# Query and key projection in other banks and with later rotary partners, and eight low halves per mixer on VectorE

## What is computed

```python
def encoder_layer(x, pos, past, lw):
    x = half_step_ffn(x, ...)
    h = rms_norm(x, lw['mix_norm_pre'])
    m, new_state = hybrid_mixer(h, pos, past, ...)
    x = x + rms_norm(m, lw['mix_norm_post'])
    x = half_step_ffn(x, ...)
    return x, new_state

def hybrid_mixer(...):
    a, g, q, k, v, qi, ki, wi = split_cols(h @ w_in)
    q = apply_rope(q, cos, sin)         # also k, qi, ki
    conv_out = conformer_conv(a, g, ...)       # a * sigmoid(g), depthwise conv, layer norm, silu
    attn_out = sparse_attention(q, qi, wi, pos, k_all, v_all, ki_all)  # top-k keys by an index score
    return concat(conv_out, attn_out) @ w_out

def apply_rope(x, cos, sin):
    x1, x2 = x[..., :half], x[..., half:]
    return concat([x1 * c - x2 * s, x2 * c + x1 * s])
```

## Time and profile before

| | us |
|---|---|
| median of 3 timed runs | 1326.3 |
| lowest, highest | 1325.33, 1329.6 |
| the profiled execution | 1322.26 |
| its span, first to last instruction | 1320.5 |
| busy in it: TensorE, VectorE, ScalarE, GpSimd | 1268.5, 790.9, 606.4, 235.6 |
| mean granted clock of TensorE | 0.982 |

### The profile page before, as it was taken

The page is one execution under the profiler, slowest core; times in us unless marked ns, Lnnn a source line. Parts: engine busy times, 40 slices in busy tenths (PEclk is TensorE's granted clock), DMA queues, the critical chain, the costliest instruction groups (busy, mean ns, idle before and its releaser), DMA issues.

```text
span 1320.5 us, 24629 instructions
## 1 busy us (share of the span) xinstructions
PE 1268.5 (96%) x9533; PEld 1197.8 (91%) x9533; DVE 790.9 (60%) x1408; ACT 606.4 (46%) x998; POOL 235.6 (18%) x150
## 2 busy tenths in 40 slices
PE   5999999998998999999999999999899899999998
PEld 4999999988757899999989999998895599999997
DVE  3666554788325776664487665457961458666543
ACT  3544444542437554444345444444423465444432
POOL 6000000455501600000040000015653062000000
PEclk9999999999989899999999999999999999999998
DMA  6354554446501355445425555453472043544541
GB/s 183 129 191 159 178 175 150 154 129 180 163 1 43 128 176 174 159 151 176 154 95 192 160 177 182 159 172 125 141 202 65 1 138 97 191 161 161 170 155 59
DMA packets 186102, 189.84 MB, mean 144 GB/s; under 512 B 9348, under 2 KB 181644, under 8 KB 186030
## 3 DMA queue, kind: packets, MB, share of 16 engines
q1 hardware_dynamic: 185230, 188.20, 44.8%
q0 software_dynamic: 416, 0.51, 0.2%
q10 hardware_dynamic: 384, 0.13, 0.0%
HBM read 179.21 MB, written 3.93 MB: 139 GB/s over the span
## 4 chain that ended last, share of the span: by engine, by line
PE 76%; DVE 10%; issue 5%; POOL 5%; ACT 2%; DMA 1%; POOLq 0%; DVEq 0%; ACTq 0%; SPq 0%
PE ps L1154 23%; PE ps L1156 22%; PE ps L1155 22%; POOL wlo L1080 5%; PE ps L1397 3%; DVE acc L761 2%; DVE x L782 2%; DVE hl L747 2%; DVE upd L774 1%; DVE wlo L737 1%; PE ps L1462 1%; ACT whi L421 1%; PE ps L1176 1%; PE ps L1432 1%; PE ps L1553 1%
## 5 line engine op out<-in xcount | busy, mean ns | idle before, releaser
L1154 PE MATMUL ps<-hh,wlo 128*128 128x288 f32 x1920 | 579.8, 302 | 10.6 <-DVE wlo L737 5.3
L1155 PE MATMUL ps<-hl,whi 128*128 128x288 f32 x1920 | 569.1, 296 | 0.0
L1156 PE MATMUL ps<-hh,whi 128*128 128x288 f32 x1920 | 567.4, 296 | 0.0
L737 DVE TENSOR_TENSOR wlo<-raw,whi 128x1024 fp32r<-128x1024 f32 (+1 forms) x269 | 322.6, 1201 | 287.1 <-ACT whi L421 283.9
L421 ACT ACTIVATE whi<-raw 128x1024 fp32r<-128x1024 f32 (+1 forms) x336 | 347.4, 1036 | 283.6 <-PE ps L1156 252.6
L1154 PEld LDWEIGHTS ps<-hh,wlo 128*128 128x128 f32 x1920 | 362.9, 189 | 18.1 <-DVE hl L747 7.1
L1155 PEld LDWEIGHTS ps<-hl,whi 128*128 128x128 f32 x1920 | 363.5, 189 | 1.3
L1156 PEld LDWEIGHTS ps<-hh,whi 128*128 128x128 f32 x1920 | 364.1, 190 | 0.0
L1080 POOL TENSOR_TENSOR wlo<-raw,whi 128x1024 fp32r<-128x1024 f32 x67 | 161.8, 2427 | 808.7 <-ACT whi L421 808.5
L1154 PE MATMUL ps<-ghi,wlo 128*128 128x288 f32 x704 | 208.4, 296 | 0.0
L1155 PE MATMUL ps<-glo,whi 128*128 128x288 f32 x704 | 207.7, 295 | 0.0
(11 more groups left out here) (200 smaller groups left out, 1013.5 us busy)
## 6 DMA issues: line engine op xcount, KB each, us to landing
raw<-in_ffn_w_up SPq DMA_DIRECT2D x88, 1024.0 KB, 5.1
raw<-in_ffn_w_down SPq DMA_DIRECT2D x32, 1024.0 KB, 5.0
raw<-in_w_in SPq DMA_DIRECT2D x24, 1024.0 KB, 5.3
raw<-in_ffn_w_down SPq DMA_DIRECT2D x16, 768.0 KB, 4.2
raw<-in_w_out SPq DMA_DIRECT2D x8, 1024.0 KB, 5.2
rep<-ext SPq DMA_DIRECT2D x64, 86.5 KB, 2.6
kc<-in_cache_k SPq DMA_DIRECT2D x2, 1024.0 KB, 7.7
vc<-in_cache_v SPq DMA_DIRECT2D x2, 1024.0 KB, 10.4
```

The costliest lines, as they stand in the source:

```text
L737: dve.tensor_tensor(wlo[:, split_slot, 0:n, :], raw[:, raw_slot, 0:n, cols], whi[:, split_slot, 0:n, :].bitcast(F32), ALU.subtract).then_i ...
L1154: pe.matmul(out, wlo[:, slot, k, :], hi, start=start, stop=False)
L1155: pe.matmul(out, whi[:, slot, k, :], lo, start=False, stop=False)
L1156: return pe.matmul(out, whi[:, slot, k, :], hi, start=False, stop=stop)
```

## The change

The query units go into banks 4 to 7 and the key units into banks 0 to 3; a table says so. The partner of a unit is issued two units later than the unit instead of one. Value unit 2 comes ahead of the first sampled logits and value unit 3 ahead of the second. ScalarE splits query unit 3 ahead of gate 2 and key unit 0 ahead of gate 3. VectorE's totals follow one round later. The low halves of output units 4 to 7 and of the next FFN's first four units are written by VectorE, each ahead of an addition to `acc`; GpSimd's two steps are gone, and so is a wait ahead of the second FFN.

```diff
+PROJ_BANK = (0, 0, 0, 4, 0, 4)
...
-                for k in range(4):
-                    split_next(G + k)
+                def gate(k):
                     act.wait_ge(glu_r, 4 * m + k + 1)
                     act.activation(bank(k), bank(k), ACT.Sigmoid).then_inc(sig_ready, 1)
 
-                for k in range(Q, V):
+                split_next(G)
+                gate(0)
+                split_next(G + 1)
+                gate(1)
+                split_next(G + 2)
+                split_next(G + 3)
+                gate(2)
+                split_next(Q)
+                gate(3)
+                for k in range(Q + 1, V):
                     split_next(k)
...
-                    if r >= 10:
-                        qk_total(r - 10)
+                    if r >= 11:
+                        qk_total(r - 11)
...
+                qk_total(6)
                 qk_total(7)
...
-                for c in range(KD - 1):
-                    add_sq(s, c, c % 2)
+                for rel in range(4):
+                    split_quad(u + U_IN + 4, 0, rel)
+                    add_sq(s, rel, rel % 2)
+                for rel in range(4):
+                    split_quad(u + U_IN + 4, 1, rel)
+                    if rel < 3:
+                        add_sq(s, 4 + rel, rel % 2)
                 residual(s, g, hq_next, g_next)
...
-                dve.wait_ge(lo_ready, ffn_unit(2 * l + 1) + 4)
...
-                step(u + U_IN + 4, 0)
-                step(u + U_IN + 4, 1)
...
-                for k in range(8):
-                    if k < 4:
-                        pe.wait_ge(u_ready, 4 * m + k + 1)
-                    else:
-                        pe.wait_ge(rope_done, 13 * m + 5 + k - 3)
-                    in_unit(Q + k, k % 4)
-                    if k:
-                        partner(5 + k - 1, (k - 1) % 4)
+                def qk_partner(k):
+                    partner(5 + k, PROJ_BANK[(Q + k) // 4] + k % 4)
+
                 pe.wait_ge(kTs_ready, 8 * m + 4)
+                in_unit(Q, 4)
+                in_unit(Q + 1, 5)
+                in_unit(Q + 2, 6)
+                qk_partner(0)
+                in_unit(Q + 3, 7)
+                qk_partner(1)
+                for k in range(4):
+                    pe.wait_ge(u_ready, 4 * m + k + 1)
+                    in_unit(K + k, k)
+                    qk_partner(2 + k)
+                pe.wait_ge(rope_done, 13 * m + 6)
                 in_unit(V, 4)
-                partner(12, 3)
+                qk_partner(6)
+                pe.wait_ge(rope_done, 13 * m + 7)
                 in_unit(V + 1, 5)
+                qk_partner(7)
...
+                pe.wait_ge(rope_done, 13 * m + 8)
+                in_unit(V + 2, 6)
                 pe.wait_ge(rope_done, 13 * m + 13)
                 pe.wait_ge(kTs_ready, 8 * m + 8)
                 logits(0)
-                in_unit(V + 2, 6)
+                in_unit(V + 3, 7)
                 logits(1)
-                in_unit(V + 3, 7)
```

More of the change, by code:

```diff
@@ L521, in save_proj @@
                     act.wait_ge(w_used, u + k + 1)
-                    act.activation(proj[:, k * T:(k + 1) * T], bank(k % 4 if k < V else 4 + k % 4),
+                    act.activation(proj[:, k * T:(k + 1) * T], bank(PROJ_BANK[k // 4] + k % 4),
                                    ACT.Copy).then_inc(proj_saved, 1)
@@ L881, in qk_products @@
                     dve.wait_ge(w_used, u + Q + k + 1)
-                    rope_products(5 + k, bank(k % 4), cosR, sinR)
+                    rope_products(5 + k, bank(PROJ_BANK[(Q + k) // 4] + k % 4), cosR, sinR)
                 def qk_total(k):
-                    rope_total(5 + k, proj[:, (Q + k) * T:(Q + k + 1) * T], k % 4)
+                    rope_total(5 + k, proj[:, (Q + k) * T:(Q + k + 1) * T], PROJ_BANK[(Q + k) // 4] + k % 4)
                 def glu_gate(k):
```

## The result

| us | before | after |
|---|---|---|
| median | 1325.8 (1324.3 to 1329.6, 4 runs) | 1309.0 (1305.6 to 1316.2, 4 runs) |
| profiled execution | 1322.3 | 1316.2 |
| its span | 1320.5 | 1314.3 |
| its mean granted clock | 0.982 | 0.978 |

The ratio is 0.9855, with a 95% interval from 0.9821 to 0.989: 16.9 us less by the medians, where the forecast said 11.4. The profiled execution of after happens to be the slowest of its four. It is 6 us faster than that of before, not 17, so the two traces can be compared place by place but not end to end.

The account below looks back on a forecast made before the run. TensorE, busy 1268.5 of 1320.5 us, bounds the kernel through its gaps and their clock cost. Mixers gain 5.6 and 5.85 us, together 11.4, so 1326.3 becomes 1314.9 us; range 1309.5 to 1320.5.

Parts of the forecast that it names:

- What bounds the kernel, and the gap: TensorE's own gaps bound it; the wait at the query partner shrinks by 3.24 and 3.2 us in the two mixers.
- The cover for value unit 0's weights: Value units: GpSimd's low half is ready at 328.62, TensorE wants it at 330.0; cover 1.4 us, the thinnest.
- What is late next?: Rest of the projection after the partner: VectorE's products, 3.88 us mask and totals fall behind nowhere.
- my walk: VectorE's order in the projection: mask 331.5 to 335.4, last total ends 338.8, sampled logits start 341.1.
- So the 1.65 us go as well, in both mixers: Partner and its unit: the half-speed clock behind the gap disappears, 1.65 us per mixer.
- So the acc wait goes and the wait for rcol takes its place: 0: Tail, last output unit to rcol broadcast: one wait replaces the other, worth 0, within -1 and +0.8 us.
- the bracket: Cited list of TensorE's waits: output unit 4's first weight tile, 0.4 us in two waits, 0.2 per mixer.
- VectorE 0.46 instead of 2.48: Additions to acc: with GpSimd idle each takes 0.46 us, where the longest took 2.48; worth little on the path.
- B, more comes back: Slow-clock stretches shorten beside tiny matmuls and the residual chain starts earlier: 4 us more gain, 1311 us; chance 0.11.
- A: Stall moves on in part, to value unit 0 or the tail: about 4 us of gain lost, 1319 us; chance 0.14.
- C: Nothing won: the partner's gap reappears later through VectorE's mask and totals; 1324 to 1327 us; chance 0.06.
- D: Slower: key 0's split delays gate 3 if its raw tile lands late; 1330 us at 7.5 us delay; chance 0.03.

Follow-up runs that it names:

- filled gap: Kernel before with seven dummy matmuls ahead of the first partner of each mixer, filling TensorE's wait: 1323.4 us, ratio 0.9952.
- before mixed: Kernel before with a quarter of convolution 2 or 3 ahead of each head of sampled values in TensorE's order: 1321.2 us, ratio 0.9947.
- the filled kernel: Before mixed plus seven dummy matmuls ahead of the first partner of each mixer: 1316.1 us, ratio 0.9908.
- the mixed pair: Two kernels with before mixed's reordering: the change with low halves left on GpSimd, 1308.4 us, and the whole change, 1304.2 us.
- rcol first: Whole change with before mixed's reordering, VectorE's low half of FFN unit 3 moved behind rcol's reciprocal: 1301.5 us, against 1303.1 without that move.
- the seven mixed profiles: Profiles of kernels with quarter convolutions ahead of the sampled values' heads: two of before, five of the change or parts; 1321.2 to 1301.5 us.

## Why the prediction was right and where it was wrong

**What bounds the kernel, and the gap: right.** 0.82 us are left of 4.07, forecast 0.83; in the second mixer 0.2 against 0.7. With value rows and keys this term was 7.74 us and measured 7.6. The cover for value unit 0's weights held: the raw tile came at 325.09 as before, and TensorE waited for no weight.

**"What is late next?": right in the result, wrong in one duration.** The mask took longer than the 3.88 us taken from the earlier trace rows. VectorE, after:

```profile
330.68 6.17 DVE L998 TENSOR_SCALAR maskS<-score 32x544 f32<-32x544 f32 x4
```

GpSimd has four low halves back to back there, from 326.23 for 9.87 us, since the value units' raw tile came late for the faster TensorE. The last totals ended 1.0 us earlier than my walk said, so it cost nothing.

**"So the 1.65 us go as well, in both mixers": the mechanism right, the size too small.** The filled gap shows the cause. The term, 3.3, measured 5.1 (5.5 unmixed). I took the length of the slow stretch from one execution, 3.4 us in both mixers; it is 3.4 or 6.8, as the earlier trace rows themselves show elsewhere (441.76 to 448.59). From the state's transposes to the value rows, filling the gap saves 1.5 us in the first mixer and 2.4 in the second, where the stretch had been 6.83. The remaining 1.2 us of the medians lie in other slow stretches (mean clock of all runs 0.985 against 0.990). The profiled pair has one: in before mixed the clock is at 0.50 from 406.85 to 410.26, across the end of the first softmax stage, where the filled kernel keeps it, and the stage with the output projection takes 1.6 us longer. That it comes from the gap is not shown.

**"So the acc wait goes and the wait for rcol takes its place: 0": the step that failed.** The prediction followed the low halves from output unit 4 to the broadcast and put what lies behind it at nothing: 0.20 us a mixer, 0.4 in all. From E, the end of the last output unit, to the broadcast it was right: in the mixed pair 2.96 and 3.16 us become 3.09 twice, since the sum of squares comes 0.7 to 0.9 us nearer to E and the new wait for rcol takes 0.85 back. The gain is on either side of that stretch. Ahead of E, output unit 4 cost 0.43 us where the bracket shows 0.20: two matmuls that start 0.13 us apart elsewhere start 0.49 apart across the wait, and the next one 0.21 later. Behind the broadcast, the residual's first addition no longer stands beside a GpSimd low half, and the next sum of x comes 0.88 us sooner. In all this is 1.2 us in the first mixer and 1.4 in the second (49.36 against 48.01), 2.5 against 0.4. The remaining 1.7 us of the 4.2 by the medians come with a higher granted clock (mean of all runs 0.990 against 0.994); that the shorter waits in the tail cause it is likely, since the filled gap did the same elsewhere, but no run shows it.

**"VectorE 0.46 instead of 2.48": right.** After, the longest addition to acc takes 0.46 us. The Trainium skill's rule that I held beside it ("SBUF — State Buffer", section "SBUF: two separate sides") agrees again with the residual's addition, 1.22 against 0.46 us. Its price there was missing from the sum.

**The rivals.** B, more comes back, was right in direction, at 17 instead of 15 us, and partly for the reason that it names (the residual chain starts sooner). A, C and D did not happen: no wait for a low half in the value units, no late gate 3.

**The range** rested on a spread of 2.5 us, and the result missed its low end by 0.6. The runs of before in these comparisons reach from 1322.3 to 1335.9, those of after from 1305.6 to 1316.2, and the softmax stage alone accounts for up to 7 us in each mixer. The slow stretches at 373.49 and 1018.6 of the old trace, 6.83 us each, already lay in that stage and would have suggested a wider one. But width alone was not the fault: 5 us below 1314.9 would be 1309.9, still above the result. The two terms above were too small, by 1.8 and 3.8 us.

## What to carry over

Follow a moved piece of work to the next point where all engines meet, not to the wait that it replaces: here a low half off GpSimd paid behind the broadcast, where the list of waits showed nothing. Price a gap of TensorE with the clock that it costs, over more than one execution. When a stage makes executions scatter, quiet it first (here by mixing tiny matmuls with large ones), and then measure the parts; and work that an engine owes to a later stage belongs behind the short instruction that another engine waits for.

## What the runs showed of the hardware

TensorE's granted clock fell to 1.2 GHz behind a gap of 3.9 to 4.1 us in six of six mixers, and behind a wait of at most 0.9 us at the same partner in none of twenty.

It also fell behind 6.8 us in which the profile has TensorE 100% busy, with tiny matmuls in it; in the changed kernel the same stage took from 54.6 to 61.7 us. With tiny and large matmuls in turn it took 55.5 us in eleven of the fourteen stretches of the seven mixed profiles, and 55.9 to 56.1 in the other three. Mixing did not end the slow stretches altogether: in five of the fourteen one of 3.41 us stands across the stage's end or right behind it. In the mixers the slow stretches of these profiles last 3.4, 6.8 or 13.65 us.

What a slow stretch costs depends on where it lies. From the broadcast to the next sum of x, with rcol first, it is 16.49 us without one and 16.47 with one of 3.41 that begins 1.2 us behind the broadcast. In the first mixer of after one of the same length begins 0.15 us behind the broadcast, and there it is 17.00 us.
